# Joining the output projection, feed-forward and gate of a hybrid decoder layer in one block

## The chip, the cores and the metric

The kernel runs on one core of one Trainium2 chip. The metric is device time in microseconds of one execution; several executions are timed and their median is given. PE is TensorE, DVE VectorE, ACT ScalarE, POOL GpSimd and SP SyncE, which issues the transfers.

## What is computed

One layer of a decoder with two mixers side by side, for 1024 prompt tokens and 64 tokens of eight decoding sequences, 1088 in all, in float32 with 1024 features:

```python
x = layer_norm(x, ln_in_g, ln_in_b)                      # h0 below
q, k, v, z, xbc, dt = split(x @ w_in)
mix = concat([dilated_attention(q, k, v), ssd(z, xbc, dt)])
h = layer_norm(ALPHA * x + mix @ w_out, ln1_g, ln1_b)
u = square(relu(h @ w_up)) @ w_down                      # 1024 -> 4096 -> 1024
h = layer_norm(ALPHA * h + u, ln2_g, ln2_b)
g = sigmoid(h @ w_gate) * (pe @ w_ple)                   # pe: 256 features per token
y = layer_norm(ALPHA * h + g, ln3_g, ln3_b)
```

## The kernel before

Every large product is made of three: both operands are split into a high part in a reduced format and the low part that remains, and hi x hi, lo x hi and hi x lo are added in PSUM. ACT makes the high part (a copy), DVE or POOL the low part (a subtraction). Tokens are worked on in nine blocks (`NB`) of 128, the last one of 64. A normalisation (`LayerNorm`) goes over three engines: DVE takes the statistics, POOL the inverse root, DVE the shift, ACT normalises (L127), POOL multiplies by the gain (L132) and DVE adds the bias (L136).

The program is a row of blocks; in each of them every engine has its own instructions in the order in which they are written, ordered against the others by semaphores, and at a block's end all engines wait for each other.

- A first block (L2058 to L2063) only loads the identity matrix, by which PE transposes, and waits for it.
- `stage_front` normalises x block by block (POOL's gain, DVE's bias), PE transposes each block (`turn_x`, L934), ACT and DVE split it (L768, L566), and PE computes three groups of 344 columns of `w_in` token by token. The weights of such a group are split by ACT (`token_hi`) and, for the low part, by DVE and POOL (`token_lo`, L571 and L448): group 0 half and half, group 1 on POOL, two parts at a time between the gains of blocks 3 to 6, group 2 on DVE. Sixteen feature-major weight blocks and the state-space mixer follow.
- `stage_attention` writes the mixed features and prefetches `w_out`.
- `stage_output` multiplies by `w_out` (L1541, `op_M`), adds the residual, normalises (LN1), and transposes each block for the next product (`op_T`, L1645). Its loops are generated by `over_blocks`, with middle rounds as a hardware loop.
- `stage_mlp` goes through 4096 hidden features in eight chunks of 4 x 128. A chunk has twelve up tiles (four weight blocks f, three token groups g of 364, 364 and 360, L1541, `ml_U`, 24 products each), ReLU on ACT, the square on POOL and ACT, and then one pass of down products over the token blocks (L1814, `ml_D`), whose sums DVE adds to the residual `R` (L1792). The last pass also splits `w_gate`: ACT's copy (L1513), DVE's low parts (L1517). The token block that is 64 rows wide has a part kept beside it that is joined at the end (L1801).
- `stage_gate` normalises `R` (LN2), copies each block on ACT to a staging tile (`gt_h`, L1922), transposes it (`gt_T`, L1964), computes the gate product (`gt_G`) and the small ple product (`gt_P`), and finishes with sigmoid, product (L1933), residual (L1935) and LN3, and the store.

Where the first down product may start, and where a stage may, is said by waits such as these:

```python
pe.wait_ge(up_lo_done, c * FB + (f + 1))      # up: weight block f is split
pe.wait_ge(staged[s], i + 1)                  # gate: the staged copy of this token block
```

## Time and profile before

| | us |
|---|---|
| median of 3 runs | 1665.02 (1664.46 to 1665.67) |
| the profiled execution, its own time | 1665.64 |
| span in its profile | 1663.7 |
| PE busy | 1550.2 (93%) |
| DVE busy | 674.0 (41%) |
| ACT busy | 499.9 (30%) |
| POOL busy | 364.3 (22%) |

The span is what the profiler sees from the first to the last instruction; the time of the same execution is 1.9 us longer. Busy shares are averages over stages with different limits. The mean clock granted to PE is 0.974 of full speed; it is below 1 in the stretches in which PE had stood still.

### The profile page before, as it was taken

What the parts mean: (1) busy time and instruction counts of PE and PEld (TensorE: products, weight loads), DVE (VectorE), ACT (ScalarE), POOL (GpSimd) and SP (SyncE); (2) the same over time, 40 slices, a digit from 0 to 9 for tenths busy, and PEclk for the clock granted to TensorE, in tenths of its full rate; (3) what the DMA queues carried; (4) which work ended last, traced back from release to release, by engine and by line L of the source; (5) the groups of instructions that cost most, each with busy time, mean ns of one, the idle gap of its engine ahead of it and who ended that gap; (6) DMA issues with size and microseconds to landing.
All of it is one profiled execution on the core that took longest, in us unless ns stands there. A gap on an engine that the chain in (4) does not pass through costs nothing. (4 is left out here: it accounts for less than half of the span.)

```text
span 1663.7 us, 23416 instructions
## 1 busy us (share of the span) xinstructions
PE 1550.2 (93%) x9164; PEld 1351.3 (81%) x9164; DVE 674.0 (41%) x1221; ACT 499.9 (30%) x952; POOL 364.3 (22%) x388
## 2 busy tenths in 40 slices
PE   4999999997899989889999999999999999986996
PEld 4899998996465668688898989889898988975884
DVE  6502664552556555533232332323233232255663
ACT  4413223453455543332130302213030221313331
POOL 6400003462343512220010201001020100102442
PEclk9999998998899999989999999999999999997998
DMA  7531112442857221121030201103020110302110
GB/s 263 162 108 33 42 51 65 160 125 83 311 191 282 103 76 38 32 81 60 3 99 1 76 25 45 56 4 97 0 76 25 47 54 10 141 12 78 48 43 32
DMA packets 104654, 134.66 MB, mean 81 GB/s; under 512 B 6912, under 2 KB 78528, under 8 KB 104192
## 3 DMA queue, kind: packets, MB, share of 16 engines
q1 hardware_dynamic: 104576, 133.60, 24.0%
q8 instruction: 52, 0.85, 0.2%
q14 instruction: 26, 0.21, 0.0%
HBM read 113.25 MB, written 20.33 MB: 80 GB/s over the span
## 5 line engine op out<-in xcount | busy, mean ns | idle before, releaser
L1541 PE MATMUL ml_U<-h1T_hi,ml_up_hi 128*128 128x364 f32 (+1 forms) x768 | 253.0, 329 | 9.1 <-PE ml_D L1814 4.8
L1541 PE MATMUL ml_U<-h1T_lo,ml_up_hi 128*128 128x364 f32 (+1 forms) x768 | 252.8, 329 | 0.0
L1541 PE MATMUL ml_U<-h1T_hi,ml_up_lo 128*128 128x364 f32 (+1 forms) x768 | 252.7, 329 | 0.0
L1727 POOL TENSOR_TENSOR ml_u<-ml_relu 128x364 f32<-128x364 f32 (+1 forms) x96 | 76.2, 794 | 654.6 <-ACT ml_relu L1744 654.6
L1744 ACT ACTIVATE ml_relu<-ml_U 128x364 f32<-128x364 f32 (+1 forms) x96 | 45.6, 475 | 568.2 <-PE ml_U L1541 568.2
L1814 PE MATMUL ml_D<-ml_down_hi,ml_u_hi 128*128 128x512 f32 x512 | 200.2, 391 | 2.4 <-DVE ml_down_lo L1784 2.4
L1792 DVE TENSOR_TENSOR R<-R,ml_D 128x512 f32<-128x512 f32 x144 | 99.0, 688 | 250.0 <-PE ml_D L1814 227.6
L1814 PE MATMUL ml_D<-ml_down_hi,ml_u_lo 128*128 128x512 f32 x512 | 199.3, 389 | 0.0
L1814 PE MATMUL ml_D<-ml_down_lo,ml_u_hi 128*128 128x512 f32 x512 | 199.3, 389 | 0.0
L1776 DVE TENSOR_TENSOR ml_u_lo<-ml_u,ml_u_hi 128x364 fp32r<-128x364 f32 (+1 forms) x96 | 49.5, 515 | 285.3 <-POOL ml_u L1727 285.3
L1541 PEld LDWEIGHTS ml_U<-h1T_hi,ml_up_hi 128*128 128x128 f32 x768 | 144.9, 189 | 12.1 <-issue 7.7
L1541 PEld LDWEIGHTS ml_U<-h1T_lo,ml_up_hi 128*128 128x128 f32 x768 | 145.0, 189 | 0.0
L1541 PEld LDWEIGHTS ml_U<-h1T_hi,ml_up_lo 128*128 128x128 f32 x768 | 144.9, 189 | 0.0
L960 PE MATMUL fr_mm<-hT_hi,fr_w_hi 128*128 128x364 f32 (+1 forms) x384 | 130.5, 340 | 0.0
L960 PE MATMUL fr_mm<-hT_hi,fr_w_lo 128*128 128x364 f32 (+1 forms) x384 | 126.7, 330 | 0.0
L960 PE MATMUL fr_mm<-hT_lo,fr_w_hi 128*128 128x364 f32 (+1 forms) x384 | 126.6, 330 | 0.0
L1814 PEld LDWEIGHTS ml_D<-ml_down_hi,ml_u_hi 128*128 128x128 f32 x512 | 96.1, 188 | 24.8 <-DVE ml_down_lo L1784 5.3
L1814 PEld LDWEIGHTS ml_D<-ml_down_hi,ml_u_lo 128*128 128x128 f32 x512 | 96.1, 188 | 20.1
L1814 PEld LDWEIGHTS ml_D<-ml_down_lo,ml_u_hi 128*128 128x128 f32 x512 | 96.1, 188 | 19.6
L1281 POOL TENSOR_TENSOR at_Z<-at_Z,at_inv 128x128 f32<-128x128 f32 (+7 forms) x64 | 72.1, 1148 | 101.1 <-DVE at_inv L1322 101.1
L960 PEld LDWEIGHTS fr_mm<-hT_hi,fr_w_hi 128*128 128x128 f32 x384 | 72.9, 190 | 1.1 <-issue 0.4
L960 PEld LDWEIGHTS fr_mm<-hT_lo,fr_w_hi 128*128 128x128 f32 x384 | 72.9, 190 | 0.2
(284 smaller groups left out, 2793.5 us busy)
## 6 DMA issues: line engine op xcount, KB each, us to landing
ml_up_raw<-in_w_up SPq DMA_DIRECT2D x32, 512.0 KB, 4.1
ml_down_raw<-in_w_down SPq DMA_DIRECT2D x32, 512.0 KB, 4.7
Kc<-in_cache_kT SPq DMA_DIRECT2D x8, 1536.0 KB, 13.8
Vc<-in_cache_v SPq DMA_DIRECT2D x8, 1536.0 KB, 10.0
fr_raw<-in_w_in SPq DMA_DIRECT2D x16, 512.0 KB, 3.9
in_x<-in_x_prompt SPq DMA_DIRECT2D x8, 512.0 KB, 6.1
h_scratch<-in_h SPq DMA_DIRECT2D x8, 512.0 KB, 3.1
sd_E<-acs_scratch SPq DMA_DIRECT2D x8, 512.0 KB, 3.9
```

The source lines that it names most:

```text
L960: last = pe.matmul(mm[:, u % 3, 0:w], wt[m % 2][:, k, :], ht[:, k, c:c + w], start=(k == 0 and part == 0), stop=(k == KD - 1 and part == 2))
L1281: pool.tensor_tensor(z, z, inv[:, m % NZ, u:u + 1].to_broadcast([P, n]), ALU.mult).then_inc(S["norm"], 1)
L1541: last = pe.matmul(out, a, b, start=(k == 0 and part == 0), stop=(k == n_k - 1 and part == 2))
L1727: pool.tensor_tensor(u[:, col:col + w], x, x, ALU.mult).then_inc(mul_done[g], 1)
L1744: act.activation(relu[:, col:col + w], pU[s][:, g, 0:w], ACT.Relu).then_inc(relu_done[s][g], 1)
L1776: last_lo = dve.tensor_tensor(u_lo[f][:, col:end], u[:, col:end], u_hi[f][:, col:end].bitcast(F32), ALU.subtract)
L1792: dve.tensor_tensor(acc, acc, pD[s][:, :], ALU.add).then_inc(added[s], 1)
L1814: last = pe.matmul(out, a, b[:, f, cols], start=(f == 0 and part == 0), stop=(f == FB - 1 and part == 2))
```

## The change

1. **Identity.** The first block is gone. `stage_front` issues the identity's transfer behind that of the first x block, and PE waits for it before its first transpose.
2. **Low parts of the token-major weights.** POOL has none any more. DVE takes the other half of group 0 in block 0, behind that block's split and ahead of the bias of block 1, and all of groups 1 and 2 behind its loop over the blocks. One semaphore, `t_lo`, counts them. The loads of group 2 and of the next weight blocks, and ACT's copies for them, come later in their queues.
3. **One block.** `stage_output`, `stage_mlp` and `stage_gate` become `stage_back`. All loops over token blocks are written out; only the six middle chunks of the feed-forward remain a loop.
   - Seam 1: the first four up tiles stand between the transposes of the output stage's blocks 7 and 8 and around the latter; the splits of the first two weight blocks are made in the last step of the output stage.
   - Seam 2: in the last down pass DVE, POOL and ACT also do LN2 of blocks 0 to 3, and PE transposes block 0 behind the fourth token block of the pass and block 1 behind the sixth. The transposes read `R` itself; the staging copy is gone. LN2 of block n + 4 is done in step n of the gate loop. `w_ple` and LN3's gain and bias are loaded behind the last down product.
   - End: LN3 of the last block is two DVE instructions (`finish_last`) in place of ACT's normalise, POOL's gain, and DVE's shift and bias.

The core of the diff:

```diff
-        with nc.Block() as block:
-            @block.sync
-            def _(sp):
-                sp.dma_start(ident[:, :], io["c_ident"]).then_inc(consts_loaded, 16)
-                sp.wait_ge(consts_loaded, 16)
...
             load_x(0)
+            sp.dma_start(ident[:, :], io["c_ident"]).then_inc(S["ident_loaded"], 16)
...
-                if n == 0:
-                    for k in range(KD // 2, KD):
-                        token_lo(0, k, S["t_lo_b"])
-                if 3 <= n < 7:
-                    for k in range(2 * (n - 3), 2 * (n - 2)):
-                        token_lo(1, k, S["t_lo_1"])
...
                 lo(n)
+                if n == 0:
+                    for k in range(KD // 2, KD):
+                        token_lo(0, k)
                 if n + 2 < NB:
                     shift(n + 2)
                 if n + 1 < NB:
                     add_bias(n + 1)
-            for k in range(KD):
-                token_lo(2, k, S["t_lo_2"])
+            for g in range(1, 3):
+                for k in range(KD):
+                    token_lo(g, k)
...
+            for n in range(NB):
+                mix_product(n)
+                if n >= 1:
+                    turn1(n - 1)
+            pe.wait_ge(S["tlo_done"], 6)
+            for f in range(2):
+                for g in range(2):
+                    if (f, g) == (1, 0):
+                        pe.wait_ge(S["x_done"], NB)
+                    if (f, g) == (1, 1):
+                        turn1(NB - 1)
+                    up(0, f, g)
+            pe.wait_ge(S["tlo_done"], NB)
+            for f in range(2):
+                up(0, f, 2)
+            for f in range(2, FB):
+                for g in range(3):
+                    up(0, f, g)
+            downs(0)
+            middle_chunks(pe, chunk)
...
+            for s in range(2):
+                for g in range(3):
+                    pe.wait_ge(relu_done[s][g], NC * 2)
+            downs(NC - 1, last_norm)
+            for n in range(NB):
+                gate_product(n)
+                if n + 2 < NB:
+                    turn2(n + 2)
+                ple_product(n)
...
+            for k in range(NB):
+                add(NC - 1, k)
+                if k == 2:
+                    dve.wait_ge(S["spilled"], 1)
+                    dve.tensor_tensor(R[0:NS, NB - 1, :], R[0:NS, NB - 1, :], relu[0:NS, 0:D], ALU.add).then_inc(S["joined"], 1)
+                if k % 2 == 0:
+                    if k >= 2:
+                        bias2(k // 2 - 1)
+                    if k < 8:
+                        statistics2(k // 2)
+                else:
+                    shift2(k // 2)
+                if k in (4, 6):
+                    turned_lo(k // 2 - 2)
+                if k >= 1:
+                    w_gate.split_lo_chunk(dve, k - 1)
...
+            def gate_hi(k):
+                act.wait_ge(w_gate.loaded, 16 * KD)
+                act.activation(w_gate.hi[:, k, :], w_gate.raw[:, k, :], ACT.Copy).then_inc(w_gate.hi_done, 1)
...
+                dve.scalar_tensor_tensor(x, x, ln3.mv[0:r, s, 0:1], ln3.G[0:r, :], ALU.subtract, ALU.mult).then_inc(S["gained"], 1)
+                dve.wait_ge(S["gained"], 1)
+                dve.wait_ge(ln3.rstd_done[s], count(n))
+                dve.scalar_tensor_tensor(x, x, ln3.rstd[0:r, s, :], ln3.B[0:r, :], ALU.mult, ALU.add).then_inc(S["finished"], 1)
```

The first place is DVE in the front, blocks 0 and 1 (`fr_t_lo` are the weights' low parts, `hT_lo` the split of a transposed block, `in_h` the normalised block):

```order
 L122 TENSOR_SCALAR in_ln_nmr<-in_ln_mv,in_ln_rstd 128x1
-L571 TENSOR_TENSOR fr_t_lo_79<-fr_t_raw,fr_t_hi_78 128x344 x4
+L531 TENSOR_TENSOR fr_t_lo_62<-fr_t_raw,fr_t_hi_61 128x344 x4
 L109 BN_STATS in_ln_bn<-in_x 128x6
 L110 BN_STATS in_ln_bn<-in_x 128x6
 L74 COPY in_ln_taken<-in_ln_bn 128x1
 L112 BN_AGGR in_ln_mv<-in_ln_bn 128x2
-L566 TENSOR_TENSOR hT_lo<-fr_T,hT_hi 128x8x128
+L526 TENSOR_TENSOR hT_lo<-fr_T,hT_hi 128x8x128
+L531 TENSOR_TENSOR fr_t_lo_62<-fr_t_raw,fr_t_hi_61 128x344 x4
 L122 TENSOR_SCALAR in_ln_nmr<-in_ln_mv,in_ln_rstd 128x1
 L136 TENSOR_TENSOR in_h<-in_h,in_ln_b 128x1024
```

Four more low parts stand between the split of block 0 and the bias of block 1.

The second place is PE at the seam from output projection to feed-forward, before (the two last transposes, then the two branches at the block's end, then the first up tile):

```order
L1541 MATMUL op_M<-op_w_hi,op_m_lo_7165 64x512
L1645 MATMUL op_T<-ident,op_h_7162 128x128 x8
L1645 MATMUL op_T<-ident,op_h_7162 128x64 x8
L1555 UNCONDITIONAL_BRANCH
L1803 UNCONDITIONAL_BRANCH
L1541 MATMUL ml_U<-h1T_hi,ml_up_hi_8114 128x364
```

and in the change, around the transposes of block 7 and then of block 8:

```order
L1496 MATMUL bk_U<-op_w_hi,bk_m_lo_7138 64x512
L1995 MATMUL bk_D<-ident,bk_h_7136 128x128 x8
L1496 MATMUL bk_U<-h1T_hi,bk_m_hi_7139 128x364
...
L1496 MATMUL bk_U<-h1T_hi,bk_m_lo_7138 128x364
L1995 MATMUL bk_D<-ident,bk_h_7136 128x64 x8
L1496 MATMUL bk_U<-h1T_hi,bk_m_hi_7137 128x364
```

Up products follow the transposes of block 7 directly; those of block 8 stand behind three up tiles, and no branch lies between.

The third place is DVE at the seam from feed-forward to gate, before: the additions of the pass's end, the weight's low parts, the join, the block's end and LN2's first statistics.

```order
L1792 TENSOR_TENSOR R_59<-R_59,ml_D1 128x512
L1517 TENSOR_TENSOR gt_wg_lo_8101<-gt_wg_raw_8099,gt_wg_hi_8100 128x1024
L1801 TENSOR_TENSOR R_59<-R_59,ml_relu_8120 64x1024
L1690 UNCONDITIONAL_BRANCH
L1927 UNCONDITIONAL_BRANCH
L109 BN_STATS gt_ln2_bn_10814<-R_59 128x6
L110 BN_STATS gt_ln2_bn_10814<-R_59 128x6
```

and in the change, from the second addition of the last down pass to the fourth:

```order
L1848 TENSOR_TENSOR R<-R,bk_D 128x512 x2
L122 TENSOR_SCALAR bk_ln_nmr<-bk_ln_mv,bk_ln_rstd 128x1
L1481 TENSOR_TENSOR bk_wg_lo<-bk_wg_raw,bk_wg_hi 128x1024
L1848 TENSOR_TENSOR R<-R,bk_D 128x512 x2
L1936 TENSOR_TENSOR R<-R,bk_relu 64x1024
L136 TENSOR_TENSOR R<-R,bk_ln_b 128x1024
L109 BN_STATS bk_ln_bn<-R 128x6
L110 BN_STATS bk_ln_bn<-R 128x6
L74 COPY bk_ln_taken<-bk_ln_bn 128x1
L112 BN_AGGR bk_ln_mv<-bk_ln_bn 128x2
L1481 TENSOR_TENSOR bk_wg_lo<-bk_wg_raw,bk_wg_hi 128x1024
L1848 TENSOR_TENSOR R<-R,bk_D 128x512 x2
```

The join, a bias and the statistics of the next block now stand between two additions of the pass.

## Rows read from the trace of the kernel before

**Rows 1.** Windows by stage: stretch, length, busy us (instructions) of PE, PEld, DVE, ACT, POOL, clock, DMA share, GB/s.

```profile
1491.40:1517.20 25.80, 3.62 (x18) 3.21 (x17) 14.61 (x24) 7.80 (x9) 7.15 (x12) 0.56 0.39 138
1517.20:1650.10 132.90, 132.90 (x598) 103.92 (x596) 74.27 (x117) 45.11 (x48) 49.51 (x43) 0.99 0.11 38
1650.10:1663.70 13.60, 0.01 (x1) 0.00 (x0) 5.39 (x8) 1.24 (x1) 3.05 (x3) 0.68 0.09 19
```

**Rows 2.** Waits of PE: what was waited for, us in total, times, longest.

```profile
PE gt_T L1964 <- ACT gt_h L1922: 22.2, 2, 14.7
```

**Rows 3.** Timeline of SP, the program's start: start, us, instruction, idle before and releaser.

```profile
0.74 0.40 SPq L2062 DMA_DIRECT2D ident<-in_c_ident  x1
2.95 0.34 SPq L314 DMA_DIRECT2D in_x<-in_x_prompt  x1
```

**Rows 4.** Timeline of DVE, front: a group of low parts, and a bias beside POOL.

```profile
15.73 1.79 DVE L571 TENSOR_TENSOR fr_t_lo<-fr_t_raw,fr_t_hi 128x344 fp32r<-128x344 f32 x4
...
38.10 1.82 DVE L136 TENSOR_TENSOR in_h<-in_h,in_ln_b 128x1024 f32<-128x1024 f32 x1
```

**Rows 5.** Timeline of PE, front: transposes of blocks 2, 3 and 8.

```profile
29.53 1.10 PE L934 MATMUL fr_T<-ident,in_h 128*128 128x128 f32 x8
...
34.45 1.09 PE L934 MATMUL fr_SS<-ident,in_h 128*128 128x128 f32 x8
...
63.29 0.71 PE L934 MATMUL fr_T<-ident,in_h 64*128 64x64 f32 x8
```

**Rows 6.** Timeline of POOL, front: a pair of low parts and the gain behind it.

```profile
37.90 2.81 POOL L448 TENSOR_TENSOR fr_t_lo<-fr_t_raw,fr_t_hi 128x344 fp32r<-128x344 f32 x2
40.66 2.40 POOL L132 TENSOR_TENSOR in_h<-in_h,in_ln_g 128x1024 f32<-128x1024 f32 x1
```

**Rows 7.** Timeline of PE: seam 1, second chunk's first products, last down pass's start.

```profile
701.08 1.04 PE L1645 MATMUL op_T<-ident,op_h 128*128 128x128 f32 x8
...
765.47 0.40 PE L1814 MATMUL ml_D<-ml_down_hi,ml_u_hi 128*128 128x512 f32 x1
...
814.37 0.43 PE L1541 MATMUL ml_U<-h1T_hi,ml_up_hi 128*128 128x364 f32 x1 [0.49 <-PE ml_D L1814]
...
862.20 0.40 PE L1814 MATMUL ml_D<-ml_down_hi,ml_u_hi 128*128 128x512 f32 x1
...
1443.61 0.40 PE L1814 MATMUL ml_D<-ml_down_hi,ml_u_hi 128*128 128x512 f32 x1
```

**Rows 8.** Timeline of ACT, last down pass: the last relu and the gate weight's copies.

```profile
1443.81 0.47 ACT L1744 ACTIVATE ml_relu<-ml_U 128x360 f32<-128x360 f32 x1 [2.93 <-PE ml_U L1541]
...
1457.61 7.70 ACT L1513 ACTIVATE gt_wg_hi<-gt_wg_raw 128x1024 fp32r<-128x1024 f32 x8 [2.41 <-DMA gt_wg_raw<-in_w_gate]
```

**Rows 9.** Timeline of DVE, end of the feed-forward: the last weight split and the join.

```profile
1492.05 1.22 DVE L1517 TENSOR_TENSOR gt_wg_lo<-gt_wg_raw,gt_wg_hi 128x1024 fp32r<-128x1024 f32 x1
1493.19 1.21 DVE L1801 TENSOR_TENSOR R<-R,ml_relu 64x1024 f32<-64x1024 f32 x1
```

**Rows 10.** The chain that ended last: start, us, engine, tile, line, count.

```profile
1517.53 11.72 PE gt_G L1541 x48
...
1532.06 0.87 PE gt_T L1964 x8
1532.93 11.20 PE gt_G L1541 x48
...
1651.46 1.23 DVE gt_wp_raw L1935
...
1655.44 1.25 ACT gt_wp_raw L127
...
1659.18 1.22 DVE gt_wp_raw L136
```

**Rows 11.** Window of DVE alone, LN2's first statistics: length, busy (instructions), clock, DMA share, GB/s.

```profile
1494.70:1496.40 1.70, 1.56 (x4) 0.50 0.38 128
```

**Rows 12.** Window behind the feed-forward's last product, columns as in rows 1.

```profile
1494.00:1496.00 2.00, 0.00 (x0) 0.00 (x0) 1.68 (x3) 0.00 (x0) 0.26 (x4) 0.66 0.14 41
```

More of the change, by code:

```diff
@@ L1679, in stage_mlp @@
-    one = lambda *names: [sem("ml_" + n) for n in names]
-    many = lambda n, k: [sem(f"ml_{n}{s}") for s in range(k)]
-    up_loaded, up_lo_done = up.loaded, up.lo_done
-    up_hi_done, down_loaded, down_hi_done, down_lo_done, down_used = one(
-        "up_hi_done", "down_loaded", "down_hi_done", "down_lo_done", "down_used")
+    ORDER = [0, NB - 1] + list(range(1, NQB))
+    early, tiles, spill, middle, small, late = (places[n] for n in ("early", "tiles", "spill", "middle", "small", "late"))
@@ L1727, in chunk, with norm2 @@
                         pool.tensor_tensor(u[:, col:col + w], x, x, ALU.mult).then_inc(mul_done[g], 1)
-            chunks(pool, chunk)
+            chunk(0)
+            middle_chunks(pool, chunk)
+            chunk(NC - 1)
+            ln2.constants(pool)
+            ln3.constants(pool)
+            def norm2(n):
+                ln2.inverse_root(pool, n % 2, n // 2, rows(n))
+                ln2.gain(pool, row(n), n % 2, n // 2, rows(n))
+            for n in range(4):
+                norm2(n)
@@ L1753, in _, with mix_hi @@
[L1753 to L1761 removed]
+            def mix_hi(n):
+                r = rows(n)
+                if n >= 2:
+                    act.wait_ge(S["mm_done"], n - 1)
+                act.activation(m_hi[n % 2][:, :, 0:r], mixT[:, :, cols(n)], ACT.Copy).then_inc(S["hi_done"], 1)
@@ new lines, in _, with statistics2 @@
+            normed_lo(NB - 1)
+            dve.wait_ge(S["spill_zeroed"], 1)
+            dve.wait_ge(S["scaled"], NB)
+            chunk(0)
+            middle_chunks(dve, chunk)
+            first_products(NC - 1, True)
+            def statistics2(n):
+                for s in range(2):
+                    dve.wait_ge(added[s], (NC - 1) * NB + ORDER.index(n) + 1)
+                if n == NB - 1:
+                    dve.wait_ge(S["joined"], 1)
+                ln2.statistics(dve, row(n), n % 2, n // 2, rows(n))
@@ new lines, in down @@
+                    pe.matmul(out, both, down_hi[:, f, half], start=(f == 0), stop=False)
+                    last = pe.matmul(out, both, down_lo[:, f, half], start=False, stop=(f == FB - 1))
+                else:
+                    a_hi, a_lo = u_hi[f][:, n * P:(n + 1) * P], u_lo[f][:, n * P:(n + 1) * P]
+                    for part, (a, b) in enumerate(((a_hi, down_hi), (a_hi, down_lo), (a_lo, down_hi))):
+                        last = pe.matmul(out, a, b[:, f, half], start=(f == 0 and part == 0), stop=(f == FB - 1 and part == 2))
@@ new lines, in chunk, with turn2 @@
+            def chunk(c):
+                for f in range(FB):
+                    for g in range(3):
+                        up(c, f, g)
+                downs(c)
+            def turn2(n):
+                s, r = n % 2, rows(n)
+                pe.wait_ge(ln2.done[s], count(n))
+                if n >= 1:
+                    pe.wait_ge(S["h_lo"], n)
+                for k in range(KD):
+                    last = pe.transpose(T2[:, k, 0:r], R[0:r, n, k * P:(k + 1) * P], ident[0:r, 0:r])
+                last.then_inc(S["h_turned"], 1)
```

810 lines of the change are left out of this document (430 added, 380 removed).

## The prediction

> **What bounds the kernel now.** I read the windows by stage first, because 93% TensorE (PE) busy over the span says nothing about the places where PE stands still. In the gate loop PE is busy for 132.90 of 132.90 us and VectorE (DVE) for only 74.27; at the seam from feed-forward to gate PE works 3.62 of 25.80 us; after the last product 13.60 us pass with PE idle [rows 1]. So inside the loops PE is the bound and work can be added to DVE freely, while at the edges everything lost is a chain of normalisation steps. The waits of PE confirm who ends it: the two transposes that open the gate stage waited 22.2 us in all for ScalarE's (ACT) staging copy [rows 2]. The first stage and the step from the output projection to the feed-forward I then read on the timeline of PE: there the question is the distance between equal instructions.
>
> **The change part by part.** All sums are against the profiled execution (1665.64 us; the median of the three runs is 0.62 lower).
>
> *Front.* The identity's transfer was issued at 0.74 and the first token block's only at 2.95, since a block of its own waited for it [rows 3]. The block goes, so everything up to the first transposes starts 2.2 us earlier; the identity now travels behind the first x transfer and is needed only when that block is normalised. Four of the low parts of group 0 come to DVE ahead of the bias of block 1. Four cost 1.79 us there [rows 4], so of the 2.2 us only some 0.6 reach the transposes of blocks 1 and 2 (29.53 becomes 28.9). Behind that the distance matters. From block 2 to block 3, where GpSimd (POOL) had no low parts, the transposes were 34.45 - 29.53 = 4.92 us apart; over the next five blocks they were (63.29 - 34.45)/5 = 5.77 apart [rows 5]. In that stretch a gain on POOL followed a pair of low parts (2.81 us), and DVE's bias took 1.82 us [rows 4, 6]. With the pairs gone from POOL I take 4.92 for all six distances: 28.9 + 6 x 4.92 = 58.4 instead of 63.29, so **-4.8**. Bounds: 2.2 if only the earlier start is kept at the end, 5.5 if also the four low parts cost nothing. The eight low parts of group 1 (3.6 us by the same price) now stand behind DVE's block loop, while PE computes that loop's last products; those of group 2 and the later weight loads are wanted some 30 us later. I cost them at nothing; if that cover is gone, PE waits up to 3.6 us once, which the range holds.
>
> *Output projection to feed-forward.* Today PE goes from the transposes of block 7 (701.08 + 1.04 = 702.12) to the first down product at 765.47, 63.35 us later; a later chunk's 288 up products take 862.20 - 814.37 = 47.83 [rows 7]. Four of the twelve up tiles need only what is ready by then, and at 47.83/12 = 3.99 us each they cover about 12 us of the last block's normalisation before PE turns it between the third and the fourth. Its transposes are 64 rows wide, about 0.65 us. If nothing stalls, the stretch is 47.83 + 0.65 = 48.5, so **-14.9**. The splits of the first two weight tiles lie on ACT and DVE while PE runs the last projections. The thinnest place is the third weight tile: its slot is free one up tile (3.99) before PE wants it, and into that must go ACT's two evictions (0.47 each by the last relu's row), ACT's copy (0.96, an eighth of 7.70 [rows 8]) and DVE's split (1.22 [rows 9]): some 0.9 are left, 0.6 after three hand-overs of 0.1. Bounds: 14.9 at best, 10.9 if PE has to wait one tile there.
>
> *Feed-forward to gate.* Today 25.80 us pass between the last down product and the first gate product [rows 1]. Now the last pass of down products, which begins at 1443.61 [rows 7], carries the normalisation of blocks 0 to 3 and both opening transposes (0.87 us each at the loop's price [rows 10]: 1.7). PE stalls in that pass as follows. It waits for the last relu, which ended at 1444.28 [rows 8]: 0.7. ACT's first gate-weight copy waits for all eight loads, as it did at 1457.61 [rows 8], 14.0 us behind the pass's start, and the first normalisation stands behind it, so its bias on DVE comes around 1463.2, after that copy (0.96), the spill copy of the same width (0.96), a normalise (1.25) and a gain (2.40) [rows 6, 10]: this holds back DVE's add for PE by 1.1 at the fourth block. There DVE has the join (1.21), the bias (1.22), statistics (1.56 busy in 1.70) and a weight split (1.22) [rows 9, 10, 11] ahead of the next add: 1.2 more at the fifth. Later steps have the chain off their path: 0.2 and 1.0 at the seventh and ninth. Sum 4.2. Behind the pass the last add, a bias and the last weight split remain; DVE began its split 0.65 us behind PE's last product [rows 1, 9], so 0.65 + 1.22 + 1.22 = 3.1. The first gate product took 11.72 at a fallen clock against 11.20 in the next [rows 10]: 0.5 comes back. 25.8 - 1.7 - 4.2 - 3.1 + 0.5 = 17.3. One unknown stands against it: DVE beside POOL. Where both subtracted or multiplied, DVE's bias took 1.82 instead of 1.22 [rows 4], 0.6 more. The join and the gain of block 0 now meet; I take 0.6 once and get **-16.7**. Bounds: 18.4 without the stall at loads and join, 9.5 if DVE is late at four blocks (first rival).
>
> The Trainium skill's page "SBUF — State Buffer", section "Who interferes with whom", says that a DVE instruction with two inputs in SBUF and a GpSimd instruction that reads SBUF share one pair of ports, and that the one that starts first holds it to its end. The trace agrees with a wait of that kind, not with a slowing in proportion: the 1.82 us bias began 0.2 us into a pair of low parts of 2.81 [rows 4, 6], and each is longer by less than one instruction of the other. By that rule the join would wait out the whole gain, of which the bias behind it had to wait anyway; the join's own 1.21 would then be lost instead of 0.6, and the sum would be 0.6 smaller.
>
> *Gate loop.* The second normalisation of later blocks moves inside it, and the staging copy goes. PE is busy throughout, a block needs 132.90/9 = 14.77 us, and DVE uses 74.27/9 = 8.25 of it [rows 1]. I cost the loop at **0**; the cover is DVE's 6.5 us of slack a block. The transfers of the ple weight start behind the last down product and are wanted one gate product, 11.2 us, later [rows 10].
>
> *Tail.* Today, behind the statistics and POOL's inverse root: an ACT normalise of 1.25 from 1655.44, a gain on POOL, a bias of 1.22 that ends at 1660.40 [rows 10]. Now two DVE instructions of the residual's kind (1.23 each [rows 10]) do it, and they stand behind the bias of block 7 (1.22), which takes about as long as the root it covers; so they run from about 1655.5 to 1658.0, and the store leaves 2.4 earlier: **-2.4**. Bounds: 1.2 if the bias is not covered, 3.6 if it costs nothing.
>
> Sum: -4.8 - 14.9 - 16.7 - 2.4 = -38.8, so 1626.8 in a profiled execution and **1626.2** as a median. Unrolled code in place of loops may cost time to load; no row of this stretch shows such a wait, and the three block entries that vanish lie inside the windows used. Bounds there: 0 and the 2.2 us of the one entry whose cost is visible [rows 3].
>
> **The rivals.** *The last pass is too tight for DVE* (0.14). The bias, statistics and split between two adds take 4.0 us, with a turned split 5.2, in steps of about 5.3 (47.8/9 by the distance 1443.61 to 1491.4); two adds need 1.3. If DVE cannot make up the delay, it is some 1.7 us more at four blocks, about +7: 1633. For it: PE reads the sums in two halves and lets DVE be late by only half a step. Against: the odd steps carry only a split, which lets it catch up.
>
> *The front does not do what it says* (0.08): if the chain hi, low, shift, bias sets 5.77 by itself, POOL's low parts were not what spread the blocks, and only the earlier start remains, less the four low parts: 3.5 to 4 are lost, 1630. Against it stands the one clean distance of 4.92.
>
> *The third up tile waits* (0.07) for its split, 3 to 4 us: 1630.
>
> *The clock* (0.07): with PE idle behind the feed-forward it was 0.66 in the mean of the 2 us from 1494.0 [rows 12], that is, it went from 2.4 to 1.2 GHz about 3 us after PE's last product. The forecast's own gap is 3.1 us. [...]
>
> *DVE becomes the bound of the gate loop, and the kernel slower* (0.02). If each of four DVE instructions a block with two SBUF inputs waited out a POOL gain of 2.40 [rows 6], and a normalise and a gain (3.65) then lay open between DVE's own steps, a block would need 8.25 + 9.6 + 3.65 = 21.5 us instead of 14.77: nine blocks give +60, so about 1687. It decides from 14.77 + 38.8/9 = 19.1 us a block. Against it: two gains last 4.8 us a block, so not all four can meet one. Tail, seams and front then stay won; it is the loop alone that turns the sign.
>
> **How the numbers follow.** The forecast has 0.62; its own range, from the bounds of seams and front taken together, is 1621.5 to 1630.5. With the rivals at 1628.5 and 1630, and most of the first one, 1620.5 to 1633.5 leaves out no more than 2 in 10. A measurement of this kernel tells a difference of 0.2%, 3.3 us, from no change; only the last rival reaches that bound or beyond on the slow side. Faster 0.97, within it 0.01, slower 0.02.
>
> **What would show it.** In the profile after: x transfer issued below 1 us; transposes of the front 4.9 us apart and the last near 58.4; between the transposes of block 7 of the output projection and the first down product about 48.5 us with no wait of PE over 0.5; in the last down pass waits of PE of 4 us in all, at the fourth, fifth and ninth block, and 3 us behind it; gate blocks at 14.8; 11 us between the last product and the end. The forecast is wrong if the front's distances stay above 5.5, if the last down pass lasts over 60 us, or if a gate block takes over 15.5.

## The result and the profile after

The changed kernel took 1627.55 us (median of 4 runs, 1625.73 to 1629.01), the kernel before 1665.27 on the same chip: a ratio of 0.977, 95% interval 0.9758 to 0.9782. The profiled execution took 1625.73, its span is 1623.9; against the profiled one of before that is 39.8 us of span, where 38.8 were forecast.

Windows by stage of the changed kernel, columns as in [rows 1]. The stretches are the front, up to the transposes of block 7 of the output projection, from there to the first down product, up to the last down pass, that pass to the first gate product, the gate loop, and the end:

```profile
0.00:60.20 60.20, 37.72 (x232) 35.85 (x232) 38.45 (x70) 28.57 (x40) 29.07 (x33) 1.00 0.67 236
60.20:697.60 637.40, 604.22 (x4337) 510.66 (x4337) 301.84 (x664) 248.91 (x586) 180.91 (x186) 0.97 0.35 116
697.60:746.80 49.20, 49.20 (x305) 48.90 (x304) 21.75 (x30) 21.75 (x34) 13.60 (x14) 1.00 0.31 96
746.80:1423.10 676.30, 668.45 (x3474) 603.68 (x3472) 198.66 (x293) 134.78 (x223) 66.55 (x84) 1.00 0.13 42
1423.10:1481.10 58.00, 50.60 (x226) 40.50 (x225) 36.84 (x56) 17.48 (x18) 15.33 (x17) 1.00 0.28 103
1481.10:1612.40 131.30, 131.28 (x596) 103.48 (x596) 70.15 (x111) 37.64 (x41) 44.81 (x39) 1.00 0.14 48
1612.40:1623.90 11.50, 0.00 (x0) 0.00 (x0) 7.53 (x9) 0.00 (x0) 2.52 (x2) 0.66 0.22 68
```

The third line is the seam to the feed-forward: PE is busy in all of it. In the kernel before it waited twice there, for the last block's normalisation and for the first split of the up weights (timeline of PE):

```profile
710.44 1.11 PE L1645 MATMUL op_T<-ident,op_h 64*128 64x64 f32 x8 [8.32 <-DVE op_h L136]
715.84 0.67 PE L1541 MATMUL ml_U<-h1T_hi,ml_up_hi 128*128 128x364 f32 x1 [4.29 <-DVE ml_up_lo L1767]
```

In the fifth line PE stands still for 7.4 of 58.0 us, where the same two pieces, the pass and the seam behind it, lasted 1517.2 - 1443.6 = 73.6. The gate loop lost no time to the work moved into it.

The front is the place that reads least like the forecast. Timeline of PE there (the transposes of blocks 0 to 3 and 8), beside [rows 5]:

```profile
15.72 1.94 PE L899 MATMUL fr_T<-ident,in_h 128*128 128x128 f32 x8 [15.72 <-DVE in_h L136]
...
24.20 1.97 PE L899 MATMUL fr_SS<-ident,in_h 128*128 128x128 f32 x8 [6.54 <-DVE in_h L136]
...
31.10 1.03 PE L899 MATMUL fr_T<-ident,in_h 128*128 128x128 f32 x8
...
35.76 1.09 PE L899 MATMUL fr_SS<-ident,in_h 128*128 128x128 f32 x8
...
60.22 0.71 PE L899 MATMUL fr_T<-ident,in_h 64*128 64x64 f32 x8
```

The distances from block 3 on are (60.22 - 35.76)/5 = 4.89 us, as forecast, but block 0 was turned at 15.72, not earlier than before (15.21), although its transfer was issued at 0.73. POOL's timeline says what it waited for, in the changed kernel:

```profile
11.97 2.34 POOL L132 TENSOR_TENSOR in_h<-in_h,in_ln_g 128x1024 f32<-128x1024 f32 x1 [5.10 <-DMA in_ln_b<-in_ln_in_b]
```

and in the kernel before:

```profile
11.56 2.34 POOL L132 TENSOR_TENSOR in_h<-in_h,in_ln_g 128x1024 f32<-128x1024 f32 x1 [2.27 <-DMA in_ln_b<-in_ln_in_b]
```

The first gain waits for the bias vector's transfer, and that landed no earlier (near 11.9, near 11.5 before) although it was issued 1.7 us earlier (2.59 against 4.29).

### The profile page after: what moved, and what is told of

The parts are those of the page before. It is cut to its first block, busy times and chain, and to the rows that moved or that the text cites. A ratio compares the mean times of both kernels' runs of the same rounds, so it can differ in the third digit from the quotient of the medians.

```text
span 1623.9 us, 23323 instructions
## 1 busy us (share of the span) xinstructions
PE 1541.5 (95%) x9164; PEld 1343.1 (83%) x9164; DVE 675.2 (42%) x1233; ACT 489.1 (30%) x942; POOL 352.8 (22%) x375
## 4 chain that ended last, share of the span: by engine, by line
PE 52%; issue 5%; DVE 3%; POOL 2%; DMA 1%; ACT 0%; SPq 0%; POOLq 0%; DVEq 0%; ACTq 0%
PE bk_U L1496 30%; PE bk_D L2016 18%; PE bk_D L1496 2%; POOL bk_u L1654 1%; PE bk_D L2011 1%; PE bk_D L2012 1%; DMA bk_wg_raw<-in_w_gate 1%; DVE bk_down_lo L1839 1%; DVE op_w_lo L1481 1%; DVE bk_m_lo L1823 1%; DVE R L1848 0%; PE bk_U L2048 0%; PE bk_D L1995 0%; POOL R L132 0%; DVE bk_wg_lo L1481 0%
## 5 line engine op out<-in xcount | busy, mean ns | idle before, releaser
L1496 PE MATMUL bk_U<-h1T_hi,bk_m_hi 128*128 128x364 f32 (+1 forms) x768 | 251.9, 328 | 4.8 <-PE bk_D L2016 4.8
L1496 PE MATMUL bk_U<-h1T_lo,bk_m_hi 128*128 128x364 f32 (+1 forms) x768 | 251.8, 328 | 0.0
L1496 PE MATMUL bk_U<-h1T_hi,bk_m_lo 128*128 128x364 f32 (+1 forms) x768 | 250.5, 326 | 0.0
L2016 PE MATMUL bk_D<-bk_down_hi,bk_u_hi 128*128 128x512 f32 x512 | 200.6, 392 | 6.5 <-DVE R L1848 3.1
L2016 PE MATMUL bk_D<-bk_down_lo,bk_u_hi 128*128 128x512 f32 x512 | 199.3, 389 | 0.0
L2016 PE MATMUL bk_D<-bk_down_hi,bk_u_lo 128*128 128x512 f32 x512 | 199.3, 389 | 0.0
L1848 DVE TENSOR_TENSOR R<-R,bk_D 128x512 f32<-128x512 f32 x144 | 98.5, 687 | 238.9 <-PE bk_D L2016 219.3
L1831 DVE TENSOR_TENSOR bk_u_lo<-bk_u,bk_u_hi 128x364 fp32r<-128x364 f32 (+1 forms) x96 | 50.9, 532 | 271.8 <-POOL bk_u L1654 271.8
L1496 PEld LDWEIGHTS bk_U<-h1T_hi,bk_m_hi 128*128 128x128 f32 x768 | 144.3, 188 | 7.8 <-issue 7.8
L1496 PEld LDWEIGHTS bk_U<-h1T_lo,bk_m_hi 128*128 128x128 f32 x768 | 144.4, 188 | 0.0
L1496 PEld LDWEIGHTS bk_U<-h1T_hi,bk_m_lo 128*128 128x128 f32 x768 | 144.1, 188 | 0.0
```

Of the source, the lines that this page charges most:

```text
L1496: last = pe.matmul(out, a, b, start=(k == 0 and part == 0), stop=(k == n_k - 1 and part == 2))
L1831: last = dve.tensor_tensor(u_lo[f][:, col:end], u[:, col:end], u_hi[f][:, col:end].bitcast(F32), ALU.subtract)
L1848: dve.tensor_tensor(acc, acc, DD[:, s, :], ALU.add).then_inc(added[s], 1)
L2016: last = pe.matmul(out, a, b[:, f, half], start=(f == 0 and part == 0), stop=(f == FB - 1 and part == 2))
```

## The experiments

All but the last two are single executions; each is read from the places that its edit touches, since the whole moves by some us with the clock (below).

**1. The pairs of low parts back on POOL.**

```diff
+                if 3 <= n < 7:
+                    for k in range(2 * (n - 3), 2 * (n - 2)):
+                        token_lo(k)
...
-            for g in range(1, 3):
-                for k in range(KD):
-                    token_lo(g, k)
+            for k in range(KD):
+                token_lo(2, k)
```

> The changed kernel with the low parts of weight group 1 back on POOL, two at a time between the gains of blocks 3 to 6; group 0 and 2 stay on DVE. Theory (the pairs made POOL the engine that spaced the blocks): from block 3 to block 8 the transposes stand 5.77 us apart again instead of 4.89, so the last one comes near 64.6 instead of 60.22, and the whole is about 4 us longer. Rival (DVE's chain or PE sets the distance, and the pairs were hidden): the last transposes stay at 60.2 within 0.5 and the time does not move.

It took 1633.89 us. Timeline of PE, transposes of blocks 3, 4 and 8:

```profile
34.70 1.09 PE L905 MATMUL fr_SS<-ident,in_h 128*128 128x128 f32 x8
...
40.23 1.09 PE L905 MATMUL fr_T<-ident,in_h 128*128 128x128 f32 x8 [0.64 <-DVE in_h L136]
...
63.57 0.71 PE L905 MATMUL fr_T<-ident,in_h 64*128 64x64 f32 x8
```

The distance is (63.57 - 34.70)/5 = 5.77, the number of before to the hundredth, and PE waits for the bias again. It was POOL's two jobs, a gain and a pair, that spaced the blocks; moving the pairs is worth five times 0.88, 4.4 us. The rival is out. The whole is 8.2 us longer than the changed kernel's profiled execution, more than the expected 4, but only 3.35 of that are in the front (63.57 against 60.22): the granted clock was also low for longer in this execution, 0.50 from 279.8 to 293.5 in the state-space part (there from 278.1 to 288.4), and it fell in the last down pass and at the first gate product, where the changed kernel's first profile has no fall (runs 11 and 12).

**2. The identity in its own block again.** The two lines of the block came back, the transfer in the front and PE's wait for it went.

> The changed kernel with the identity loaded and waited for in a block of its own again, everything else as changed. Theory (the first gain waits for the bias vectors, which land with the whole burst of first transfers, so an earlier start of the burst is lost in it): the first transposes, at 15.72 in the changed kernel, come at 15.2 to 15.8, the time stays within 0.7 us. Rival (the earlier start was kept and something else ate it): the first transposes come 2.2 us later, near 17.9, and the whole is 2 us longer.

It took 1627.47 us. Timelines of SP, POOL and PE, the first x transfer, the first gain and the transposes of block 0:

```profile
3.00 0.34 SPq L284 DMA_DIRECT2D in_x<-in_x_prompt  x1
```

```profile
12.04 2.35 POOL L132 TENSOR_TENSOR in_h<-in_h,in_ln_g 128x1024 f32<-128x1024 f32 x1 [2.60 <-DMA in_ln_b<-in_ln_in_b]
```

```profile
15.70 1.97 PE L898 MATMUL fr_T<-ident,in_h 128*128 128x128 f32 x8 [15.70 <-DVE in_h L136]
```

Block 8 was turned at 59.44. Runs 1, 3 and 4, on the same chip and with the early start, turned block 0 at 15.21, 15.67 and 15.78. Starting 2.2 us earlier is worth nothing that can be seen; the theory holds.

**3. The four moved low parts behind the bias of block 1.**

```diff
                 lo(n)
-                if n == 0:
-                    for k in range(KD // 2, KD):
-                        token_lo(0, k)
                 if n + 2 < NB:
                     shift(n + 2)
                 if n + 1 < NB:
                     add_bias(n + 1)
+                if n == 0:
+                    for k in range(KD // 2, KD):
+                        token_lo(0, k)
```

> The changed kernel with the four moved low parts of group 0 behind the bias of block 1 on DVE instead of ahead of it. Theory (they sit in the chain to the transposes of block 1): those come 1.7 us earlier, 22.5 instead of 24.20, and the last ones of the front 1.2 to 1.7 us earlier than 60.22. Rival (PE needs these low parts as early as the bias, so the wait only changes its name): PE waits inside the products of block 0 for them, the transposes of block 2 stay at 31.1 and the last ones at 60.2.

It took 1625.92 us. Block 1 was turned at 22.45, as the theory says, but block 2 at 30.16 and block 8 at 59.57. On DVE the four low parts now took 3.96 us instead of 1.79 beside POOL's gain, and PE waited 1.36 for the bias of block 2. From block 0 to block 8 it is 43.90 us; the kernels whose front is the changed one's show 43.96 to 45.10. So 1.7 us were won at block 1 and most or all of them were lost at block 2: neither expectation describes it.

**4. The last transposes of the output projection ahead of all up products.**

```diff
-            pe.wait_ge(S["tlo_done"], 6)
-            for f in range(2):
-                for g in range(2):
...
-                    if (f, g) == (1, 1):
-                        turn1(NB - 1)
-                    up(0, f, g)
+            turn1(NB - 1)
             pe.wait_ge(S["tlo_done"], NB)
```

> The changed kernel with the transposes of the output projection's last block ahead of all up products, and these in their plain order; the block stays one block. Theory (the four up tiles cover the normalisation of the last block): PE waits 8.3 us for it again, as before the change, and some 1 to 2 us more for the split of these transposes, so the stretch from the transposes of block 7 to the first down product is 57 to 59 us instead of 48.2 and the whole 9 to 11 us longer. Rival (most of the 15 us came from the block boundary and the early weight loads): the stretch grows by less than 4 us.

It took 1642.29 us. Timeline of PE at the seam:

```profile
708.13 1.11 PE L1995 MATMUL bk_D<-ident,bk_h 64*128 64x64 f32 x8 [9.38 <-DVE bk_h L136]
...
710.65 0.67 PE L1496 MATMUL bk_U<-h1T_hi,bk_m_hi 128*128 128x364 f32 x1 [1.41 <-DVE h1T_lo L1813]
```

The two waits are 10.8 us, half a us above the theory's. The stretch from the transposes of block 7 (698.74) to the first down product (760.35) is 61.6, 13.4 more than in the changed kernel and above the theory's 57 to 59: the first up products behind the waits start at the lower clock, 0.67 us for one as against 0.43 [rows 7], which I had left out. The granted clock was 0.50 from 701.7 to 715.3 here and from 706.2 to 719.8 in the kernel before; in the changed kernel, without the waits, it was 1.00. So the four up tiles, with the clock that they keep up, carry the seam's gain; by subtraction 1 to 2 us of the 15 are left for the barrier and the early weight loads, which no run takes apart.

**5. The first normalisation of the last down pass ahead of the gate weight's first copy on ACT.**

```diff
-                if k < KD:
+                if k == 1:
+                    gate_hi(0)
+                if 1 <= k < KD:
                     gate_hi(k)
```

> The changed kernel with ACT's first copy of the gate weight behind the normalisation of token block 0 in the last down pass instead of ahead of it. Theory (the copy waits for all eight loads and holds the first normalisation back): PE's waits of 0.49 and 1.81 us at the fourth and fifth block of that pass go, at most 0.5 us is left of them, and the rest of the pass is as it was; 1.8 to 2.3 us shorter. Rival (DVE simply has too much to do between two additions: join, bias, statistics, weight split): the wait at the fifth block stays above 1.2 us.

It took 1624.42 us. The waits at the fourth and fifth block became 0.64 and 0.79, from 0.48 and 1.81: 0.9 us of the 1.8 to 2.3 expected. POOL's and DVE's timelines at that place, first the gain, then the join:

```profile
1437.85 2.40 POOL L132 TENSOR_TENSOR R<-R,bk_ln_g 128x1024 f32<-128x1024 f32 x1 [6.28 <-DMA bk_ln_b<-in_ln_b]
```

```profile
1438.75 2.58 DVE L1938 TENSOR_TENSOR R<-R,bk_relu 64x1024 f32<-64x1024 f32 x1
```

ACT's copy was out of the way, and the next in line ended last: the normalisation's bias vector, which is issued behind the gate weight's eight loads. The gain that it released then held the join up: it took 2.58 us where it takes 1.21 by itself, and it ended 1.1 behind the gain. The theory is half right, and the rival was not met either.

**6. PE waits for the gate weight by eighths.**

```diff
-                if n == 0:
-                    pe.wait_ge(w_gate.lo_done, KD)
+                def ready(k):
+                    if n == 0:
+                        pe.wait_ge(w_gate.lo_done, k + 1)
```

> The changed kernel with PE's first gate product waiting for each eighth of the split gate weight by itself instead of all eight at its start. Theory (the idle 3.14 us behind the last down product are the chain of last addition, bias and last weight split): the gap shrinks to below 0.3 us, since the last eighth is wanted only some 5 us into the product, and the gate stage starts 2.8 to 3.1 us earlier. Rival (something else is wanted at the same time, for instance PE's slots or the weights of the ple product): the gap moves into the product or to the ple product and less than 1 us is won.

It took 1623.08 us, with a fall of the clock in the pass. Timeline of PE, the first gate product, in the changed kernel and in this run:

```profile
1481.09 0.47 PE L1496 MATMUL bk_U<-bk_wg_hi,bk_m_hi 128*128 128x512 f32 x1 [3.14 <-DVE bk_wg_lo L1481]
```

```profile
1478.43 0.47 PE L1496 MATMUL bk_U<-bk_wg_hi,bk_m_hi 128*128 128x512 f32 x1 [0.30 <-PE bk_D L2016]
```

Neither this product nor the ple product behind it waits. The theory holds.

**7. The bias of block 7 ahead of the last block's multiplication.**

```diff
+                if n == NB - 1:
+                    bias3(n - 1)
                 gated(n)
...
-                if n >= 1:
+                if 1 <= n < NB - 1:
                     bias3(n - 1)
```

> The changed kernel with the bias of block 7's last normalisation ahead of the last block's gate multiplication on DVE, where DVE stands idle, instead of between its statistics and its last two instructions. Theory (DVE's instructions with two inputs in SBUF hold up POOL's inverse root: its two small steps took 1.06 and 1.47 us there instead of 0.19 and 0.54): the first small step still meets the first of the two last DVE instructions and takes over 0.8, the second step runs free at 0.54, and the end comes 0.7 to 1.0 us earlier (11.5 us from PE's last product to the end becomes 10.5 to 10.8). Rival (POOL was slow for a reason of its own): both steps stay long, and the last DVE instruction waits for them 1.5 us; the gain is under 0.3.

It took 1627.06 us in all, since the clock fell at two places in this execution (below); the tail itself is 10.63 instead of 11.57, as the theory has it. Timeline of POOL, inverse root of the last block, in the changed kernel:

```profile
1616.64 1.06 POOL L116 TENSOR_TENSOR bk_ln_veps<-bk_ln_mv,bk_ln_eps 64x1 f32<-64x1 f32 x1 [9.03 <-DVE bk_ln_mv L112]
1617.77 1.47 POOL L118 TENSOR_TENSOR bk_ln_rstd<-bk_ln_veps,bk_ln_mhalf 64x1 f32<-64x1 f32 x1
```

and in this run:

```profile
1618.91 0.18 POOL L116 TENSOR_TENSOR bk_ln_veps<-bk_ln_mv,bk_ln_eps 64x1 f32<-64x1 f32 x1 [9.02 <-DVE bk_ln_mv L112]
1619.17 1.39 POOL L118 TENSOR_TENSOR bk_ln_rstd<-bk_ln_veps,bk_ln_mhalf 64x1 f32<-64x1 f32 x1
```

One hold-up went with the bias, one stayed with the first of the last two instructions. It stayed on the second step, not on the first as I had written, but the sum is what was expected.

**8. The split tiles 736 bytes lower.** One line: `- 736` behind the start address of the four tiles.

> The changed kernel with the four tiles that hold the split up weights (and the split mixed features, and the split blocks of the gate stage) 736 bytes lower in SBUF, where their start has the same remainder by 2048 as before the change (640 instead of 1376). Theory (the address of the stationary tiles sets the small difference in the distance of the up products, 96.65 us a middle chunk against 96.95 before): a middle chunk takes 96.95 again, the gate blocks 14.87 instead of 14.74, the whole is 2 to 3 us longer. Rival (the difference has another cause): chunks stay at 96.65 and gate blocks at 14.74.

It took 1626.25 us. Timeline of PE, first down products of two successive middle chunks:

```profile
936.71 0.40 PE L2016 MATMUL bk_D<-bk_down_hi,bk_u_hi 128*128 128x512 f32 x1
...
1033.67 0.40 PE L2016 MATMUL bk_D<-bk_down_hi,bk_u_hi 128*128 128x512 f32 x1
```

They are 96.96 us apart, where the changed kernel has 96.64 to 96.70 and the kernel before 96.93 to 96.98; gate blocks took 14.82 instead of 14.74. So the address of the stationary tiles is the cause in the feed-forward, and of half of the difference in the gate loop. The whole did not get longer: over the output projection, whose tiles moved with these, the same shift won some 2.3 us: a token block took 11.77 to 11.81 us instead of 12.07. That part was not expected.

**9. Another order of the first loads.** Gain and bias vectors went directly behind the first x block; ACT's weight copies and all eight of DVE's low parts went behind block 1.

```diff
-            for k in range(KD // 2):
-                token_lo(0, k)
...
+            lo(0)
+            add_bias(1)
+            for k in range(KD):
+                token_lo(0, k)
+            statistics(2)
+            shift(2)
```

> The changed kernel with another order at the very start: gain and bias vectors directly behind the first x block, then identity, second x block, weights; ACT normalises block 1 and splits block 0 ahead of its weight copies, and DVE makes all eight low parts of group 0 behind the bias of block 1. Theory (the first gain waits for the bias vector, which lands as a late part of the burst, and the work on the weights stands ahead of the first blocks in their queues): the bias vector lands by 9.5 instead of 11.9, the first transposes come at 11.5 to 13.5 instead of 14.4 to 15.8, the second below 20 instead of 22.9 to 24.3, and the last of the front at 54 to 57.5 instead of 58.7 to 60.5. Rival (the transfers of the burst share the bandwidth and all land near its end, whatever their order): the first transposes stay above 14 and the last above 58.

It took 1632.27 us, which is slower. Timeline of PE, transposes of blocks 0 to 2:

```profile
12.73 1.94 PE L899 MATMUL fr_T<-ident,in_h 128*128 128x128 f32 x8 [12.73 <-DVE in_h L136]
...
18.59 1.97 PE L899 MATMUL fr_SS<-ident,in_h 128*128 128x128 f32 x8 [3.92 <-DVE in_h L136]
...
30.56 1.97 PE L899 MATMUL fr_T<-ident,in_h 128*128 128x128 f32 x8 [5.06 <-DVE in_h L136]
```

The theory of the loads holds for block 0, 3.0 us earlier; block 1 came 5.6 earlier, with the low parts out of its way as well. But the statistics of block 2 now stood behind the eight low parts, and PE waited 5.06 us for that block's bias. Behind that wait the granted clock fell:

```profile
30.60:36.60 6.00, 6.00 (x23) 6.00 (x24) 4.35 (x8) 2.74 (x4) 3.17 (x4) 0.50 0.60 204
```

Block 2 was still turned 0.5 us earlier than in the changed kernel, but block 3 at 38.06 instead of 35.76, and the front's last transposes came at 62.51. The order of the loads does move the start; my order on DVE threw it away, by the wait and by the lower clock behind it.

**10. Together: 5, 6, 7 and 9, with the normalisation's vectors between the gate weight's loads.**

> The changed kernel with the start of the run on the first loads, the first normalisation of the last down pass ahead of ACT's gate-weight copies (with the gain and bias vectors of that normalisation now between the gate weight's transfers instead of behind them), PE's waits for the gate weight by eighths, and the earlier bias at the end. Theory: PE's waits in the last down pass are 1.0 at its first block and below 0.5 each behind it but for 0.8 at the ninth, no gap over 0.4 us behind it, 10.6 us from PE's last product to the end; the clock stays at 1.00 through pass and gate stage, since no gap of PE there is over 1.1 us; in all 8 to 11 us below the changed kernel's 1625.7 to 1629.0, so 1616 to 1619.5. Rival (the gains are given back where the next chain ends, above all the fourth and fifth block of the pass with the join waiting for POOL's gain): above 1621.

It took 1627.51 us, which is no better than the changed kernel. The front brought 9's loss along. In the pass the waits at the fourth and fifth block grew into one of 3.51 us: with two transfers among them the eight loads were all there only at 1443.1, and DVE's first weight split, which is ahead of the third addition, waited 6.22 for ACT's copy. Behind that wait the clock fell (0.50 in the 2 us from 1446.1); in the gate stage it stayed at 1.00. The rival was right on the time.

**11 and 12. The changed kernel again, and one that gives DVE's light steps the splits**, five executions of each on one chip. 12 has the edits of 5, 6 and 7 and this:

```diff
-                    if k >= 2:
+                    if 2 <= k < 8:
                         bias2(k // 2 - 1)
...
-                if k >= 1:
-                    w_gate.split_lo_chunk(dve, k - 1)
+                if k in (3, 5, 7):
+                    for j in (k - 3, k - 2):
+                        w_gate.split_lo_chunk(dve, j)
+            for j in (KD - 2, KD - 1):
+                w_gate.split_lo_chunk(dve, j)
+            bias2(3)
```

> The changed kernel itself once more, beside the next run on the same chip. Theory (the clock falls in some executions behind PE's stall of 1.8 us in the last down pass and in most of them behind the gap of 3.1 us at its end, 1.5 to 1.6 us each): the times lie in steps of about 1.6 us between 1625.5 and 1629.5, most of them at 1627.5 and above, a median of 1627 to 1628.5. Rival (the spread has another source, the transfers at the start): the times are spread evenly, and a run with a clock of 1.00 in the gate stage is no shorter.

> The changed kernel with ACT's first normalisation ahead of the gate-weight copies, PE's waits for the gate weight by eighths, the earlier bias at the end, and DVE's splits of the gate weight moved to the steps of the last down pass that carry no statistics (two each at the fourth, sixth and eighth block, two behind the pass, ahead of the last bias). The front is the changed kernel's. Theory (DVE was late at the steps with join or bias, statistics and a split, and PE's two long gaps let the clock fall): PE's waits in the pass behind its first block sum to less than 1 us instead of 3.1, the gap behind it is below 0.4, no fall of the clock in pass or gate stage, 10.6 us of tail; 6 to 9 us below the run beside it, 1618.5 to 1621. Rival (the waits come back at the steps with two splits, or the first eighth of the weight is late for them): less than 5 us.

The changed kernel took 1626.87 us (1625.76 to 1627.92), ratio to before 0.9759, interval 0.9746 to 0.9773. Run 12 took 1618.38 (1618.10 to 1618.59), ratio 0.9710, interval 0.9696 to 0.9723: 8.5 us below the run beside it, and the best of this study. PE's waits in its last pass, from the view of waits, first the changed kernel, then this one:

```profile
PE bk_U L1496 <- DVE bk_wg_lo L1481: 3.1, 1, 3.1
PE bk_D L2016 <- DVE R L1848: 3.1, 3, 1.8
...
PE bk_D L2016 <- issue: 1.1, 1, 1.1
```

```profile
PE bk_D L2024 <- issue: 1.0, 1, 1.0
...
PE bk_D L2024 <- DVE R L1850: 0.7, 1, 0.7
```

What is left is the wait for the last relu and one addition, with a gap of 0.30 behind the pass; the tail is 10.62. From the pass's first product to the first gate product it is 50.9 us instead of 56.9 to 58.5. Between the two profiled executions, 9.5 us apart, the waits inside the pass behind its first block give 2.5, the gap 2.8, the clock 3.1 and the tail 0.95; the front of run 12 took 0.8 longer. What the moved splits give without the other three edits was not run.

The clock: in the profile of run 11 PE's waits (1.07, 0.50, 1.81, 0.80 and 3.14) are within 0.02 us those of the changed kernel's first profile, but the granted clock behind them is not. Windows of run 11 behind the wait of 1.81 and behind that of 3.14:

```profile
1447.40:1449.40 2.00, 2.00 (x6) 1.57 (x7) 1.77 (x3) 1.33 (x2) 0.00 (x0) 0.58 0.00 0
1449.40:1451.40 2.00, 2.00 (x7) 1.56 (x6) 0.00 (x0) 2.00 (x3) 1.95 (x1) 0.56 0.00 0
...
1481.80:1483.80 2.00, 2.00 (x5) 1.63 (x6) 0.00 (x0) 0.03 (x1) 0.00 (x0) 0.52 1.09 365
1483.80:1485.80 2.00, 2.00 (x7) 1.54 (x7) 0.94 (x1) 2.00 (x3) 0.00 (x0) 0.63 0.96 266
```

The same places in the first profile:

```profile
1448.30:1450.30 2.00, 2.00 (x9) 1.66 (x10) 1.77 (x3) 1.33 (x2) 0.00 (x0) 1.00 0.00 0
...
1481.10:1483.10 2.00, 2.00 (x9) 1.64 (x10) 0.00 (x0) 0.36 (x1) 0.00 (x0) 1.00 1.04 333
```

Near 0.5 is the lower of the two levels, 1.2 GHz. The first fall cost 58.53 - 56.89 = 1.6 us of the pass, the second 16.40 - 14.90 = 1.5 of the first gate block. Of the ten profiles with the 3.14 us gap nine have a first gate block of 16.1 to 16.5 and one, the changed kernel's first, has 14.90; of the three with the gap closed (6, 10, 12) all have 14.9. Behind the wait of 1.81 us it fell in six of the ten profiles that have that wait. The times do not lie in the clean steps that I had expected, their median is 0.1 below the expected 1627 to 1628.5, and only one of the five is above 1627.5, since the front moves by up to 1.4 us too (block 0 was turned between 14.40 and 15.78 in the changed kernel and in the runs that leave its first loads as they are); but with the long waits closed five runs lie within 0.5 us.

## Why the prediction was right, and where not

The time, 1626.2 forecast and 1627.55 measured, is in the forecast's own range. By its steps, on the profiled execution:

- **Front, -4.8 forecast, -3.1 measured** (63.29 to 60.22). The step that failed is "so everything up to the first transposes starts 2.2 us earlier". Run 2 shows no gain from the earlier start, run 9 that the order of the first transfers sets it. The four low parts then cost their 1.7 us in full at block 1 (24.20, and 22.45 without them in run 3, which started alike). The sum was also wrong by itself: 2.2 less 1.79 is 0.4, not 0.6, and with the low parts at nothing it gives 6.4, not the bound of 5.5. The other step, 4.92 instead of 5.77 us a block, is shown by run 1.
- **Output projection to feed-forward, -14.9 forecast, -15.1 measured**: 698.63 to 746.85 is 48.2, 48.5 forecast. Run 4 shows the interleaved tiles to be the cause of 13.4 of it. The third weight tile never waited.
- **Feed-forward to gate, -16.7 forecast, -15.6 measured** up to the first gate product; the 0.5 us that this product was to win back, counted in the -16.7, come on top and lie in the gate loop's line. The two waits of 14.75 and 7.44 us for the staged copy are gone; that it is the overlap that took them away is read from the traces, since no run puts the normalisation back behind the pass. PE's waits in the pass were 1.06, 0.48, 1.81 and 0.80, together 4.15 against 4.2, and the gap behind it 3.14 against 3.1. The parts came out otherwise, so that the sum agrees by luck: the relu cost 1.06 instead of 0.7, the fourth block 0.48 instead of 1.1, the fifth 1.81 instead of 1.2, the seventh nothing instead of 0.2 and the ninth 0.80 instead of 1.0. Run 5 shows that ACT's copy was one link in that chain and the bias vector the next, run 12, which changed DVE's order and ACT's together, that the waits behind the first block can be brought to 0.7 us.
- **Join against gain**, 0.6 taken: the join began at 1440.30, 0.12 us before the gain, which took 3.35 instead of 2.40. The Trainium skill's "SBUF — State Buffer", section "Who interferes with whom", lets the one that starts first hold the ports to its end. Here that was the join, and in run 5 the gain, when the join took 2.58 instead of 1.21. The trace agrees both times to some 0.15 us: the waits are 0.95 and 1.37, where the other instruction still had 1.09 and 1.50 to go. They are not the 0.6 I had taken from one row.
- **Gate loop, 0 forecast**: no wait of PE in it. Its blocks took 14.74 instead of 14.88 us, 1.1 us over eight distances, half of which run 8 puts down to the tiles' address.
- **Tail, -2.4 forecast, -2.1 measured.** What is short is the sentence that the bias takes about as long as the inverse root it covers: beside DVE's bias and the instruction behind it POOL's root took 2.5 us, and the last instruction waited 0.51 for it. The bias could have stood in DVE's idle time before (run 7, 0.94 us). That the two instructions in place of four are the gain is read from the trace and was not tried.
- **Not forecast**: the middle of the feed-forward, 678.1 to 676.3 us, -1.85, by the tiles' address (run 8); and 0.4 us between the front and the output projection. There the granted clock was 0.50 from 279.5 to 293.2 before and from 278.1 to 288.4 after. The four runs that have the longer low stretch (1, 2, 9 and 10) took 638.3 to 638.9 us from the front's last transposes to those of block 7, the eight profiles with the shorter one and the tiles where they were 637.0 to 637.6, and the kernel before 637.8; so the clock is argued from the traces, not tried, and does not give the 0.4 by itself. PE did not stand still ahead of this fall: it was in 32 products of 32 rows by 256 columns, 11.43 us in the kernel before, so the sentence that the clock is below 1 where PE had stood still does not hold for this stretch.

Front, pass and tail fell short of the forecast by 1.7, 0.6 and 0.3 us, and 3.4 us came from places where none had been forecast (the middle of the feed-forward, the gate blocks, these 0.4). That the two nearly cancel, and the span is only 1.0 us below its forecast, is luck; that each of the four places gained within 1.7 us of its forecast is not.

Of the rivals, the clock's, at 0.07, is what the median shows: the first profile, which happened to have no fall, is 1.1 us faster than its forecast, and the median, with a fall in most of the profiles, 1.35 slower. The mean clocks of the four executions agree with it: 0.986 at 1625.73, 0.984 at 1627.53 and 1627.56, 0.983 at 1629.01. I read the gap of 3.1 us against a fall 3 us behind PE's last product and gave it too little. The rival's 1628.5 is 2.3 above the forecast; no run shows that price, a fall cost 1.5 to 1.6. The second fall, behind the wait of 1.81 us, no rival had. By its last sign, a gate block of over 15.5, the forecast would have been wrong in nine of ten profiles: the first gate block took 16.1 to 16.5 in them, by the clock, while the others took 14.74. DVE being late at four blocks did not happen: it was late at the fourth, fifth and ninth. The loop never came near DVE's bound.

## What to carry to other kernels

When a load is issued earlier, look first at what releases the work behind it: if that is the last of a burst of transfers, as it was here, the order in the burst can be worth more than its beginning (3.0 us against nothing that could be seen). When a stage's tail is laid under another stage's products, distribute it by what each step of the covering loop has left; a sum that fits is not enough: here the steps with a join or statistics were the late ones, and the weight splits fitted into the others. The gap of 3.1 us cost another 1.5 when the clock fell behind it, in nine of ten profiles, so closing it was worth more than its length.

## What was not expected of the hardware

- The distance of up products depends on where the stationary tiles lie in SBUF: a middle chunk takes 96.65 us with a start that leaves 1376 by 2048 and 96.95 with 640, and the same move had the opposite sign in the output projection. What in the address decides is open.
- DVE and POOL hold each other up over very small operations too: two POOL steps of one element a partition took 1.06 and 1.47 us instead of 0.19 and 0.54 beside DVE instructions with two inputs in SBUF, and four low parts on DVE 3.96 instead of 1.79 beside a gain.
- With the same instructions and the same waits the clock fell behind a PE wait of 1.8 us in some executions and not in others.
